# Grouping the decay functions of a GLA layer and moving five other steps of a hybrid decoder kernel

## The reference

```python
def rms_norm(x, g):
    y = x * lax.rsqrt(jnp.mean(x * x, axis=-1, keepdims=True) + EPS)
    return y * g

def gla_mixer(hn, w_in, w_gk2, b_gk, g_out, w_out, s0):
    proj = hn @ w_in                        # q, k, v, g and a rank-16 part for the decays
    gk = jax.nn.log_sigmoid(proj[..., i4:] @ w_gk2 + b_gk) / GATE_NORM
    o, s = gla_chunked(q, k, v, gk, s0)
    o = rms_norm(o, g_out) * jax.nn.silu(g)
    return o @ w_out, s

def gla_chunked(q, k, v, gk, s0):           # chunks of 64 tokens
    b = jnp.cumsum(gc, axis=3)              # within a chunk
    q_in, k_in = qc * jnp.exp(b), kc * jnp.exp(-b)
    att = jnp.where(causal, jnp.einsum('bhnik,bhnjk->bhnij', q_in, k_in), 0.0)
    o_intra = jnp.einsum('bhnij,bhnjv->bhniv', att, vc)
    chunk_kv = jnp.einsum('bhnck,bhncv->bhnkv', kc * jnp.exp(b_last - b), vc)
    # the state of each chunk: decay[c] * state + chunk_kv[c]; o_inter = q_in @ state
```

## Time and profile before

| | |
|---|---|
| median of 3 runs | 1081.63 us (1079.15 to 1083.99) |
| profiled execution, its own time | 1082.17 us |
| its span | 1080.4 us |
| mean granted clock of TensorE | 0.941 |
| busy: TensorE / VectorE / ScalarE / GpSimd | 89% / 60% / 37% / 23% |

### The profile page before, as it was taken

How to read it: one execution, slowest core, us unless ns; L and a number is a source line. 1 busy time by engine, 2 the same in 40 slices (tenths; PEclk the granted TensorE clock), 3 DMA queues, 4 the chain that set the end, 5 groups by cost and what they waited for, 6 DMA issues and landing times.

```text
span 1080.4 us, 14938 instructions
## 1 busy us (share of the span) xinstructions
PE 963.2 (89%) x5249; PEld 655.3 (61%) x5249; DVE 645.3 (60%) x755; ACT 396.2 (37%) x1259; POOL 250.6 (23%) x133
## 2 busy tenths in 40 slices
PE   6899876788888987999896989999999999899994
PEld 3566555667764433554345868877754444499893
DVE  4553225876765789798997541222248677655544
ACT  5302236322333554566544231112243333244323
...
GB/s 278 334 251 324 338 195 39 182 168 122 123 107 208 318 316 228 249 225 294 297 321 286 41 4 313 324 297 312 291 226 264 233 224 198 204 79 78 79 1 80
DMA packets 111163, 228.27 MB, mean 211 GB/s; under 512 B 7249, under 2 KB 70328, under 8 KB 111088
## 3 DMA queue, kind: packets, MB, share of 16 engines
...
...
## 4 chain that ended last, share of the span: by engine, by line
PE 53%; DVE 16%; DMA 8%; ACT 6%; issue 5%; POOL 2%; SPq 1%; ACTq 0%; POOLq 0%; DVEq 0%
PE pp L1443 16%; PE pp L1446 8%; PE pp L1824 6%; DVE slot L1133 5%; PE pp L1428 4%; PE pp L1783 4%; DMA slot<-in_cache_k_dram 4%; PE pp L1808 3%; DMA w_raw<-in_gla_w_in_dram 3%; DVE zall L1134 3%; ACT slot L721 2%; PE pp L1797 2%; POOL slot L549 2%; PE pp L1833 1%; DVE rstd L1006 1%
## 5 line engine op out<-in xcount | busy, mean ns | idle before, releaser
L549 POOL TENSOR_TENSOR slot<-slot,qb 128x1024 f32<-128x1024 f32 x80 | 216.0, 2719 | 233.2 <-DMA slot<-in_cache_k_dram 192.0
L978 DVE TENSOR_TENSOR w_lo<-w_raw,w_hi 128x1024 fp32r<-128x1024 f32 x58 | 78.1, 1350 | 107.0 <-ACT w_hi L606 107.0
L1134 DVE TENSOR_REDUCE zall<-slot 128x16 f32<-128x1024 f32 x104 | 125.2, 1216 | 20.8 <-POOL slot L549 19.2
L721 ACT ACTIVATE slot<-slot 128x64 f32<-128x64 f32 x384 | 91.8, 241 | 30.8 <-POOL slot L549 30.8
L1446 PE MATMUL pp<-xa_hi,w_hi 128*128 128x512 f32 x200 | 86.4, 432 | 12.9 <-DVE w_lo L978 12.9
L1133 DVE TENSOR_TENSOR slot<-slot,qb 128x1024 f32<-128x1024 f32 x48 | 90.2, 1879 | 1.8 <-DMA slot<-in_cache_k_dram 1.8
L1431 PE MATMUL pp<-xn,w_unsplit 128*128 128x512 f32 x192 | 87.3, 609 | 3.8 <-DVE q1T L1001 3.8
L1431 PE MATMUL pp<-xn,w_raw 128*128 128x512 f32 x192 | 86.3, 601 | 4.8 <-ACT xn L617 4.1
L606 ACT CAST w_hi<-w_raw 128x1024 fp32r<-128x1024 f32 x58 | 60.3, 1043 | 75.3 <-PE pp L1446 40.5
L1443 PE MATMUL pp<-xb_hi,w_hi 128*128 128x260 f32 x384 | 80.4, 291 | 5.3 <-DVE w_lo L978 5.3
L1446 PE MATMUL pp<-xa_lo,w_hi 128*128 128x512 f32 x200 | 82.4, 412 | 0.0
...
## 6 DMA issues: line engine op xcount, KB each, us to landing
slot<-in_cache_k_dram SPq DMA_DIRECT2D x128, 512.0 KB, 5.2
slot<-in_cache_v_dram SPq DMA_DIRECT2D x128, 512.0 KB, 5.4
...
slot<-in_gla_w_in_dram SPq DMA_DIRECT2D x24, 512.0 KB, 10.4
...
slot<-in_gla_w_out_dram SPq DMA_DIRECT2D x8, 512.0 KB, 7.4
```

Of the source, the lines that this page charges most:

```text
L549: nc.gpsimd.tensor_tensor(slot[s][:], slot[s][:], qb[:, (n // NPG) % 2, :], ALU.mult).then_inc(S("k_mul_pool"), 1)
L721: ins = nc.scalar.activation(part, part, ACT.Copy, accum_out=zall[:, n % NPG, b * SH + h:b * SH + h + 1])
L978: nc.vector.tensor_tensor(lo, raw, hi.bitcast(F32), ALU.subtract).then_inc(S("w_split"), 1)
L1134: nc.vector.tensor_reduce(zall[:, n % NPG, b * SH:(b + 1) * SH], at.rearrange("p (h d) -> p h d", d=HD), AX.X, ALU.add).then_inc(S("k_used ...
```

## The change

- The decays of all heads go through each function together: Abs and Exp of four heads at u = 1 (`decays_size`), Ln of four heads at u = 2, `decays_exp` of two heads each at u = 3 and 4; VectorE's `decays_sum` for two heads each at u = 2 and 3, `decayed` at u = 4 and 5. gE has four buffers, gD lies in the second half of gT; VectorE's first sum waits for the store of the sampled tokens' states (`ss_out`).
- `queries_at` comes ahead of the decays on ScalarE.
- `gla_states` is issued in two halves, the first ahead of `gla_square_sum`.
- The root `rms(1)` moves to the last wo0 job, ahead of the page sum, the reciprocal between two parts of the page reductions, and the last squares of norm 1 ahead of `up_tile0(1)`.
- Scores and weights go back one job later (i = 2, 3 and 6, 7), the running product at i = 4.
- The first key job's low half has a buffer of its own, in the space of `work`; its high half waits for g1's sixth product alone, and both halves come ahead of job 7's other steps.
- GpSimd leaves out the eighth square; TensorE adds it with a second pair of matmuls.

In the diff below a line of "..." marks what is left out.

```diff
--- before.py
+++ after.py
@@ -287 +287 @@
         states = new("states", [P, NCH, HV])
-        gE, gD = ([at(f"{n}{i}", [P, NP_TOK], F32, off_states + (2 * i + e) * size([P, NP_TOK])) for i in range(2)]
-                  for e, n in enumerate(("gE", "gD")))
+        gE = [at(f"gE{h}", [P, NP_TOK], F32, off_states + h * size([P, NP_TOK])) for h in range(GH)]
+        gD = [gT[:, GH + h, :] for h in range(GH)]
@@ -314 +314 @@
         slot += [at(f"slot{4 + i}", [P, D], F32, off_slots + (1 + i) % 4 * D * 4) for i in range(4)]
+        w_lo_k0 = at("w_lo_k0", [P, 1024], F32R, off_work)[:]
@@ -369 +370 @@
 
+            lo = w_lo_k0 if j == PHASES["K"][0] else w_lo[j % 2][:]
             return (raw_pair(j // 2)[:, :, P * (j % 2):P * (j % 2) + P],
-                    w_hi[j % 2][:].rearrange("p (k n) -> p k n", k=KT),
-                    w_lo[j % 2][:].rearrange("p (k n) -> p k n", k=KT))
+                    w_hi[j % 2][:].rearrange("p (k n) -> p k n", k=KT), lo.rearrange("p (k n) -> p k n", k=KT))
@@ -529 +530 @@
 
+                if n % KT == KT - 1:
+                    return
@@ -536 +539 @@
                 else:
-                    pool.wait_ge(S("sq_added"), n - 3 * KT)
+                    pool.wait_ge(S("sq_added"), n - 3 * KT - (n - 3 * KT) // KT)
@@ -599 +602 @@
                 if j >= 2:
-                    act.wait_ge(S("mm"), tiles_through(PHASES["K"][0] - 1 if unsplit(j - 2) else j - 2))
+                    act.wait_ge(S("mm"), tiles_through(PHASES["K"][0] - 3 if unsplit(j - 2) else j - 2))
@@ -618 +621 @@
                 if n >= 3 * KT + 2:
-                    act.wait_ge(S("sq_added"), n - 3 * KT - 1)
+                    norm, tile = (n - 2) // KT - 3, (n - 2) % KT
+                    if tile == KT - 1:
+                        act.wait_ge(S("ss_mm"), norm + 1)
+                    else:
+                        act.wait_ge(S("sq_added"), (KT - 1) * norm + tile + 1)
@@ -733 +740 @@
 
-            def decays_ln(h):
-
-                if h == 0:
-                    act.wait_ge(S("s_used"), S_WIDE)
-                if h >= 2:
-                    act.wait_ge(S("kdec"), h - 1)
-                e = gE[h % 2]
-                act.wait_ge(S("gk_out"), h + 1)
-                own.then(nc.scalar.activation(e[:], gkT[:, h, :], ACT.Abs))
-                own.then(nc.scalar.activation(e[:], e[:], ACT.Exp, scale=-1.0))
-                nc.scalar.activation(e[:], e[:], ACT.Ln, bias=1.0).then_inc(S("gk_ln"), 1)
+            def decays_size():
+
+                act.wait_ge(S("s_used"), S_WIDE)
+                act.wait_ge(S("gk_out"), GH)
+                for h in range(GH):
+                    own.did(nc.scalar.activation(gE[h][:], gkT[:, h, :], ACT.Abs))
+                own.wait()
+                for h in range(GH):
+                    own.did(nc.scalar.activation(gE[h][:], gE[h][:], ACT.Exp, scale=-1.0))
+
+            def decays_ln():
+
+                own.wait()
+                for h in range(GH):
+                    nc.scalar.activation(gE[h][:], gE[h][:], ACT.Ln, bias=1.0).then_inc(S("gk_ln"), 1)
...
                 nc.scalar.activation(dec[:, h, :], gkT[:, h, CH - 1:NP_TOK:CH], ACT.Exp, scale=1 / GATE_NORM)
-                nc.scalar.activation(gE[h % 2][:], gkT[:, h, :], ACT.Exp, scale=1 / GATE_NORM)
-                own.did(nc.scalar.activation(gD[h % 2][:], gD[h % 2][:], ACT.Exp, scale=1 / GATE_NORM))
+                nc.scalar.activation(gE[h][:], gkT[:, h, :], ACT.Exp, scale=1 / GATE_NORM)
+                own.did(nc.scalar.activation(gD[h], gD[h], ACT.Exp, scale=1 / GATE_NORM))
...
                 v_rows(u - 1)
-                if 2 <= u < 2 + GH:
-                    decays_exp(u - 2)
-                if 1 <= u <= GH:
-                    decays_ln(u - 1)
                 queries_at(PHASES["v"][0] + u)
+                if u == 1:
+                    decays_size()
+                elif u == 2:
+                    decays_ln()
+                elif u in (3, 4):
+                    decays_exp(2 * u - 6)
+                    decays_exp(2 * u - 5)
@@ -832 +846 @@
                         embedding(c, 1 + c, pT0, bank[4 + c])
+                if u == 7:
+                    rms(1)
...
                 loads_at(j)
-                if u == 0:
-                    rms(1)
@@ -908 +922 @@
                         sum_page(j)
+                    if i == 7:
+                        split_hi(j + 1)
...
                     sigmoid_tile(16 + i, g1T[:, i, :], work[:, 2 + i % 2, :])
-                    if i in (1, 2):
-                        sample_sigmoids(2 * i - 2)
-                        sample_sigmoids(2 * i - 1)
+                    if i in (2, 3):
+                        sample_sigmoids(2 * i - 4)
+                        sample_sigmoids(2 * i - 3)
...
                         x_hi(4 * KT + 2 * i - 7, hT[:, 2 * i - 7, :])
-                    if i in (5, 6):
-                        sample_weights_out(2 * i - 10)
-                        sample_weights_out(2 * i - 9)
-                if i >= 7:
+                    if i in (6, 7):
+                        sample_weights_out(2 * i - 12)
+                        sample_weights_out(2 * i - 11)
+                if i >= 8:
@@ -1140 +1156 @@
                     dve.wait_ge(S("masks"), 1)
-                own.then(nc.vector.scalar_tensor_tensor(g, g, 0.0, gE[h % 2][:], ALU.min, ALU.subtract))
+                    dve.wait_ge(S("ss_out"), 16)
+                own.then(nc.vector.scalar_tensor_tensor(g, g, 0.0, gE[h][:], ALU.min, ALU.subtract))
...
                 chunks = g.rearrange("p (c n) -> p c n", n=CH)
-                nc.vector.tensor_tensor(gD[h % 2][:].rearrange("p (c n) -> p c n", n=CH),
+                nc.vector.tensor_tensor(gD[h].rearrange("p (c n) -> p c n", n=CH),
...
                 dve.wait_ge(S("gk_e"), h + 1)
-                nc.vector.tensor_tensor(qT[:, h, :], qT[:, h, :], gE[h % 2][:], ALU.mult)
+                nc.vector.tensor_tensor(qT[:, h, :], qT[:, h, :], gE[h][:], ALU.mult)
                 nc.vector.tensor_tensor(gkT[:, h, :], gkT[:, h, :], kT[:, h, :], ALU.mult)
-                nc.vector.tensor_tensor(kT[:, h, :], kT[:, h, :], gD[h % 2][:], ALU.mult).then_inc(S("kdec"), 1)
+                nc.vector.tensor_tensor(kT[:, h, :], kT[:, h, :], gD[h], ALU.mult).then_inc(S("kdec"), 1)
@@ -1163 +1180 @@
                 score_pages(j)
-                if 3 <= u < 3 + GH:
-                    decayed(u - 3)
-                if 1 <= u <= GH:
-                    decays_sum(u - 1)
+                if u in (2, 3):
+                    decays_sum(2 * u - 4)
+                    decays_sum(2 * u - 3)
+                if u in (4, 5):
+                    decayed(2 * u - 8)
+                    decayed(2 * u - 7)
@@ -1241 +1260 @@
                 add_residual(j, u)
-                score_pages(j)
+                score_pages(j, 0, 2)
+                if u == 7:
+                    recip(1)
+                score_pages(j, 1, 2)
...
                 j = PHASES["ple0"][0] + u
-                if u == 0:
-                    recip(1)
@@ -1273 +1293 @@
                 if i >= 8:
+                    split_lo(j + 1)
+                if i == 7:
@@ -1291 +1313 @@
                     normed(j, work[:, 2 + u % 2, :])
-                if i == 7:
-                    split_lo(j + 1)
...
                     sample_gate(done)
-                if i == 3:
+                if i == 4:
@@ -1487 +1507 @@
 
-                pe.wait_ge(S("sq_added"), KT * (i - 2))
+                n = (i + 1) * KT - 1
+                pe.wait_ge(S("sq_added"), (KT - 1) * (i - 2))
                 for t in range(2):
-                    last = nc.tensor.matmul(pp[3][:, t, 0:H2], ones[:], sqacc[:, t * H2:(t + 1) * H2],
-                                            start=True, stop=True)
+                    nc.tensor.matmul(pp[3][:, t, 0:H2], ones[:], sqacc[:, t * H2:(t + 1) * H2],
+                                     start=True, stop=False)
+                pe.wait_ge(S("sq"), n + 1)
+                for t in range(2):
+                    last = nc.tensor.matmul(pp[3][:, t, 0:H2], ones[:], work[:, n % 2, t * H2:(t + 1) * H2],
+                                            start=False, stop=True)
@@ -1652 +1677 @@
 
-            def gla_states(h):
-
-                pe.wait_ge(S("kd_out"), h + 1)
-                if h:
-                    pe.wait_ge(S("o_out"), h)
-                for c in range(NCH):
+            def gla_states(h, chunks):
+
+                if chunks[0] == 0:
+                    pe.wait_ge(S("kd_out"), h + 1)
+                    if h:
+                        pe.wait_ge(S("o_out"), h)
+                for c in chunks:
@@ -1697 +1723 @@
                 else:
+                    gla_states(h, range(4))
...
                         gla_square_sum(h - 1)
-                    gla_states(h)
+                    gla_states(h, range(4, NCH))
@@ -1725 +1752 @@
                 product(PHASES["ple0"][0] + u, 2 * KT, wait_x=(u == 0))
```

(18 more changed lines are left out.)

## The result

Over 20 executions of each kernel, the changed kernel takes 1074.43 us (1068.24 to 1082.19) against 1081.76 us (1076.4 to 1090.35): ratio 0.9929, 95% interval [0.9909, 0.995], a gain of 7.7 us by the ratio and 7.3 by the medians. It is faster by more than 0.5%, as forecast, but by less than half of the 18.4 us, and the time lies 0.4 us above the range. The profiled execution took 1071.41 us. A ratio leaves out executions that take over 1.5% more than the fastest of their kernel, which matters for the experiments e4 (two of five left out, ratio 0.983, by the medians of all 0.989) and e10 (two of six, 0.983 and 0.988).

The account below looks back on a forecast made before the run. TensorE, busy nine tenths of the span, was taken as the bound, with time to gain where it stalls or runs slowly. 11 + 0 + 0.8 - 0.5 + 6.8 + 0.3 = 18.4 us gave 1063.6 us, range 1056 to 1074.

Parts of the forecast that it names:

- Part 1: Value stage: grouped decays and earlier queries, three table loads instead of nine, gain 11 us, between 9.6 and 13.7.
- the walk: Step-by-step dating of the value stage's new order, up to the first gate product at 201.7 to 205.8 us.
- The price of a stall: TensorE products started after a wait: up to 1.93 us beyond the wait itself, by matmuls at the lower clock.
- Rival (d): Value steps 2 to 5: VectorE's two-input instructions stretched beside GpSimd's page multiplies, up to 2.1 us each; slower; chance 0.03.
- Rival (a): Gate stage or page ring keeps its own pace, Part 1 leaves 3 us or less: 1072 to 1075; chance 0.10.
- Rival (c): ScalarE's nine table loads stay, Part 1 falls to about 4 us: 1071 us; chance 0.04.
- Rival (b): First key product gains nothing, its halves or last activations being late: 1070.6 us; chance 0.07.
- Part 5: First key product: its 5.29 us wait and 1.5 us of slow clock go, gain 6.8 us, between 3.5 and 7.3.
- Part 4: Scores and weights back one product later: the 6.42 us wait stays, -0.5 us, between -1 and +0.5.
- Part 2: States in two halves, first ahead of the square sum: not waited for, 0 us, between -1 and +2.
- Part 3: Second norm's root moved earlier: 2.1 us lost, 3.0 saved on page multiplies, +0.8 us, between -2 and +1.5.
- Part 6: Last squares: GpSimd's addition ahead of the matmul goes, two matmuls added in the norm before; +0.3 us, -1 to +1.3.

Follow-up runs that it names:

- e4: The changed kernel, with GpSimd multiplying only 64 of 1024 columns of the value stage's ten pages: ratio 0.9831 to the kernel before.
- e10: The changed kernel with value products' halves one step earlier, decayed products one head a step, and ple1's gate norm back to one matmul pair: 1069.53 us, ratio 0.9834.
- light pages: The changed kernel, GpSimd multiplying only 64 of 1024 columns of the value stage's ten pages, run a second time: 1058.93 us, ratio 0.9791 to the kernel before.

## Why the prediction was wrong, by its steps

**Part 1** is the step that failed: 11 us in the walk, between 9.6 and 13.7; measured 0 in A, 1.5 to 2.5 in the mean. The walk allowed 0 to 4.2 us of stretching in the first pair of sums and none by name afterwards ("four or so" in all). The first broadcast begins at 160.88, 2.25 us later than in the kernel before; with that taken off, against the walk:

| start of | walk | measured | before |
|---|---|---|---|
| product 4 | 173 to 177 | 177.1 | 176.7 |
| product 5 | 180 to 183.4 | 185.4 | 187.81 |
| product 6 | 188 to 190.7 | 193.1 | 201.69 |
| product 7 | 196 to 198.5 | 206.7 | 209.4 |
| first gate product | 201.7 to 205.8 | 215.5 | 215.4 |

Three errors add up. The sums ended at 175.9, at the stretched end of their bound. Product 4 then started after a wait of 7.49 us and took 8.1 us, eleven of its 24 matmuls at the lower clock; the walk left it and its transposes 6.4 us before product 5, enough at the full clock only. (The walk's date for low half 5, 178 to 182, also leaves out low half 4 and a normalization, 1.9 us: it was ready at 184.0.) And at product 6, where 8.6 us of the lead over before were still there, the walk went on at 8.4 us a step with every decayed product at 0.68; three of six were stretched, the step took 13.6 us, and product 7, 8.6 us long behind its wait, took the rest. The old order wins it back because it starts product 7 without a wait. The price of a stall was set too low as well: 1.93 us was the difference of 7.51 and 5.58 us, of which the second starts only where the transposes end. From first to last matmul a product at the full clock takes 5.8 us, so the price was 1.7 there, and it was 2.3 and 2.8 us behind the longer waits here.

**Rival (d)** named the mechanism and its place, at a chance of 0.03, and priced it by a count: nine stretched instructions beyond the walk's before the gain is gone. Five in all, one more than the walk's four, cost part 1 its whole gain. They were the sign that the prediction had set down for being wrong; of its signs for being right, product 5 before 184 and a first gate product near 204 failed with them. The price of a stretched instruction is not its 2.1 us but what stands behind it, here a low half that TensorE waits for, and then the clock. **Rival (a)** gave the right size (1072 to 1075) by the wrong way: neither the gate stage nor the ring is seen to give anything back (B is 111.0 against 110.3), and with light pages what A gains, 14.3 us, arrives at the end (14.9, give or take 6). **Rival (c)** is out: three loads, at 145.31, 166.94 and 172.53. **Rival (b)** is out:

```profile
627.70 1.23 DVE L994 TENSOR_TENSOR w_lo_k<-w_raw,w_hi 128x1024 fp32r<-128x1024 f32 x1 [0.47 <-ACT w_hi L609]
...
632.49 3.22 DVE L1003 SCALAR_TENSOR_TENSOR xb_lo<-hT,gcol,xb_hi 128x520 fp32r<-128x520 f32 x2 [1.33 <-ACT xb_hi L620]
```

**Part 5** was right: the low half is there at 628.9, the last low activations at 635.7, product K0 runs from 631.06 to 636.95 without a pause. 6.8 us were forecast, 5.6 measured for it alone. **Part 4**, -0.5: D gives 6.4 us on the mean for parts 4 and 5 together, so no loss shows; the wait for g1's first evacuation stayed, as said, at 6.88 us (6.42 before).

**Part 2**, 0: right. The second half of the states waits as before:

```profile
264.29 1.13 PE L1690 MATMUL pp<-vtok,kdtok 64*128 64x256 f32 x8 [2.54 <-DVE states L1203]
```

**Part 3**, +0.8: right within what can be told, and by its mechanism. VectorE waits for the root and then multiplies its two pages unstretched, 1.23 and 1.22 us for 3.27 and 2.13:

```profile
417.88 3.35 DVE L1022 RECIPROCAL rstd<-rstd 128x512 f32<-128x512 f32 x1 [1.95 <-ACT rstd L640]
421.27 1.23 DVE L1149 TENSOR_TENSOR slot<-slot,qb 128x1024 f32<-128x1024 f32 x1
...
423.67 1.22 DVE L1149 TENSOR_TENSOR slot<-slot,qb 128x1024 f32<-128x1024 f32 x1
```

From the residual at 413.65 to the first normed gate tile at 426.05 it is 12.4 us, 13.3 before (411.51 to 424.84). **Part 6**, +0.3: the last square goes straight to TensorE (a wait of 1.38 us at 1050.01, 3.61 before), and VectorE waits 2.71 us for the last root instead of 4.15. Two more matmuls stand before ple1's root. Parts 2, 4 and 6 were not tried alone. The ends of parts 2, 3, 4 and 6 add up to -5 and +5.3, not -4 and +5, so that the forecast's own upper end was 1074, not 1073; the result lies outside either.
